# A masked decay on VectorE, whole-chunk weight splits on GpSimd, and earlier decode queries in a hybrid decoder layer

## The reference

```python
h = rmsnorm(x); p = h @ w_in        # q-latent | kv-latent | rope key | z | x,B,C | dt | gates
A = mla_attend(...)                 # 16 heads, causal for the prompt, over 2048 cached positions for samples
# SSD branch, 32 heads in 8 groups of 4, chunks of 128 tokens
cs = cumsum(dt * a)                 # per chunk and head
decay = exp(where(tri, cs[l] - cs[s], -inf))
y_diag = (C B^T * decay) @ (x * dt)
state  = state * exp(cs_end) + B^T (x * dt * exp(cs_end - cs))
y_off  = C @ state * exp(cs)        # samples: one step with exp(dt * a) and dt
B_out = rmsnorm_by_group((y + D x) * silu(z))
mix = (sigmoid(ga) * (A @ w_a) + sigmoid(gb) * (B_out @ w_b)) @ w_out
x = x + rmsnorm(mix);  x = x + rmsnorm(w_down relu(w_up rmsnorm(x))^2)
```

## Time and profile before

| | |
|---|---|
| time, median of 3 runs | 1741.69 us (1738.41 to 1745.32) |
| profiled execution, own time | 1741.69 us |
| its span, first to last instruction | 1739.9 us |
| TensorE busy, mean granted clock | 1517.3 us (87%), 0.913 of full speed |
| VectorE busy | 893.5 us (51%) |
| ScalarE busy | 512.4 us (29%) |
| GpSimd busy | 586.4 us (34%), of it line 413: 574.3 us, 736 instructions, 811 ns each |
| GpSimd idle before line 413, waiting for ScalarE's rounding | 1106.1 us |
| TensorE line 572, 256 instructions | 36.9 us busy |
| TensorE line 623, 64 instructions | 12.3 us busy |

### The profile page before, as it was taken

The page is one execution under the profiler, slowest core; times in us unless marked ns, Lnnn a source line. Parts: engine busy times, 40 slices in busy tenths (PEclk is TensorE's granted clock), DMA queues, the critical chain, the costliest instruction groups (busy, mean ns, idle before and its releaser), DMA issues.

```text
span 1739.9 us, 29329 instructions
## 1 busy us (share of the span) xinstructions
PE 1517.3 (87%) x11936; PEld 1405.3 (81%) x11936; DVE 893.5 (51%) x1794; ACT 512.4 (29%) x930; POOL 586.4 (34%) x748
## 2 busy tenths in 40 slices
PE   5799989899797997989987688998993999999995
PEld 4798778788686887878876467878993999999995
DVE  5566677666675776757767432221336222222225
ACT  3232323323233232332332222222222322222221
POOL 2353332233322323324231012323443454544541
PEclk9898989899898998998988688997995999999997
DMA  3133122122221212212213059863320223223221
GB/s 111 61 94 96 49 80 68 46 88 63 78 73 41 88 61 85 77 44 87 63 44 106 4 179 286 270 206 115 126 95 13 83 88 97 86 98 97 86 98 61
DMA packets 109592, 160.51 MB, mean 92 GB/s; under 512 B 16498, under 2 KB 83571, under 8 KB 109459
## 3 DMA queue, kind: packets, MB, share of 16 engines
q1 hardware_dynamic: 56594, 130.14, 23.1%
q10 hardware_dynamic: 52864, 28.51, 5.8%
HBM read 145.87 MB, written 12.74 MB: 91 GB/s over the span
## 4 chain that ended last, share of the span: by engine, by line
PE 72%; DVE 18%; ACT 3%; issue 3%; ACTq 1%; SPq 1%; POOL 1%; DMA 1%; DVEq 0%; POOLq 0%
PE lin L456 53%; PE lin L631 2%; PE Pb L487 2%; PE lin L495 2%; PE Pb L543 2%; PE lin L605 2%; DVE acc L1467 1%; PE Pb L552 1%; PE lin L572 1%; ACTq L1027 1%; PE Pb L584 1%; PE Pb L587 1%; PE Pb L559 1%; DVE arena L1281 1%; DVE arena L1363 1%
## 5 line engine op out<-in xcount | busy, mean ns | idle before, releaser
L413 POOL TENSOR_TENSOR w_lo<-w_stage,w_hi 128x256 fp32r<-128x256 f32 x736 | 574.3, 811 | 1106.1 <-ACT w_hi L826 1106.1
L456 PE MATMUL lin<-act_hi,w_hi 128*128 128x260 f32 x1760 | 373.5, 295 | 22.2 <-DVE acc L1535 10.8
L456 PE MATMUL lin<-act_lo,w_hi 128*128 128x260 f32 x1760 | 362.1, 288 | 0.0
L456 PEld LDWEIGHTS lin<-act_hi,w_hi 128*128 128x128 f32 x1760 | 279.5, 195 | 31.8 <-issue 24.5
L456 PEld LDWEIGHTS lin<-act_lo,w_hi 128*128 128x128 f32 x1760 | 280.7, 195 | 0.0
L826 ACT ACTIVATE w_hi<-w_stage 128x1024 fp32r<-128x1024 f32 x184 | 193.9, 1054 | 257.4 <-PE lin L456 221.1
L456 PE MATMUL lin<-mid_hi,w_hi 128*128 128x260 f32 x1024 | 218.7, 296 | 34.1 <-DVE mid_lo L1456 18.8
L456 PE MATMUL lin<-act_hi,w_lo 128*128 128x260 f32 x1760 | 233.4, 285 | 0.0
L456 PEld LDWEIGHTS lin<-act_hi,w_lo 128*128 128x128 f32 x1760 | 219.5, 189 | 3.3 <-issue 3.3
L456 PE MATMUL lin<-mid_lo,w_hi 128*128 128x260 f32 x1024 | 214.1, 292 | 0.0
L456 PEld LDWEIGHTS lin<-mid_hi,w_hi 128*128 128x128 f32 x1024 | 166.7, 199 | 44.8 <-issue 35.8
(11 more groups left out here) (238 smaller groups left out, 2006.5 us busy)
## 6 DMA issues: line engine op xcount, KB each, us to landing
w_stage<-in_wall SPq DMA_DIRECT2D x184, 512.0 KB, 3.7
arena<-in_cache SPq DMA_DIRECT2D x124, 144.0 KB, 3.2
arena<-in_state ACTq DMA_DIRECT2D x16, 512.0 KB, 7.5
out_stateT<-arena ACTq DMA_DIRECT2D x16, 512.0 KB, 4.0
o_attn<-in_cache SPq DMA_DIRECT2D x64, 128.0 KB, 3.6
o_attn<-in_cache ACTq DMA_DIRECT2D x64, 128.0 KB, 3.9
arena<-in_xT SPq DMA_DIRECT2D x8, 520.0 KB, 5.6
out_yT<-arena SPq DMA_DIRECT2D x8, 260.0 KB, 2.0
```

The source lines that it names most:

```text
L413: low = pool.tensor_tensor(w_lo[:, slot, part], w_stage[:, slot, part], w_hi[:, slot, part].bitcast(F32), ALU.subtract)
L456: mm = pe.matmul(lin[:, pl.slot, hf, 0:HALF], w[:, ch.slot, off:off + P], r[:, hf * HALF:(hf + 1) * HALF], start=(k == 0 and p == 0), stop ...
```

## The change

It has three parts. First, GpSimd's split of a chunk is one instruction of 1024 columns in place of four of 256. Second, the head rows are no longer picked by matmuls against `ident`: VectorE multiplies `cs3`, repeated four times, by the one-hot columns of the group's heads into `csm` (32x512, one per scan chunk) and `sdm` (32x64, one per group), and one matmul against ones spreads them. The mask of chunk c + 1 is made at the end of VectorE's `scan_front(c)`, the first one and `sdm` at the group's start. Third, in a decode row `queries(b + 1)` stands before `row_out(b - 1)`.

```diff
@@ semaphores csm_ready, sdm_ready; tiles @@
+        csm = sb("csm", [SSM_HEADS, HPG, CHUNK])
+        sdm = sb("sdm", [SSM_HEADS, HPG, 16])
@@ gpsimd, split @@
-                        for q in range(4):
-                            part = slice(256 * q, 256 * q + 256)
-                            low = pool.tensor_tensor(w_lo[:, slot, part], w_stage[:, slot, part],
-                                                     w_hi[:, slot, part].bitcast(F32), ALU.subtract)
-                        low.then_inc(S["w_split"], 1)
+                        pool.tensor_tensor(w_lo[:, slot, :], w_stage[:, slot, :], w_hi[:, slot, :].bitcast(F32),
+                                           ALU.subtract).then_inc(S["w_split"], 1)
@@ tensor, scan_front(c) @@
+                    pe.wait_ge(S["csm_ready"], g * 4 + (c + 1))
-                    for h in range(HPG):
-                        pe.matmul(lin[:, pl.slot, 0, h * P:(h + 1) * P], head_row(h), cs3[:, tok], start=True, stop=True)
+                    pe.matmul(lin[:, pl.slot, 0, :], ones[0:32, :], csm[:, :, :], start=True, stop=True)
@@ tensor, decode decays @@
-                if g:
-                    pe.wait_ge(S["state_ready"], g * 4)
-                else:
-                    pe.wait_ge(S["rows_ready"], 1)
-                    pe.wait_ge(S["sp_ln"], 2)
-                for h in range(HPG):
-                    mm = pe.matmul(Pb[:, 3, 16 * h:16 * h + 16], head_row(h), cs3[:, SEQ:SEQ + 16], start=True, stop=True)
-                mm.then_inc(S["sdec_mm"], 1)
+                pe.wait_ge(S["sdm_ready"], g + 1)
+                pe.matmul(Pb[:, 3, 0:64], ones[0:32, :], sdm[:, :, :], start=True, stop=True
+                          ).then_inc(S["sdec_mm"], 1)
@@ vector, group @@
+                onehot = ident[0:32, bass.ds(g * 4, 4)]
+
+                def masked_decay(c):
+                    dve.tensor_tensor(csm[:, :, :], repeat(cs3[:, CHUNK * c:CHUNK * (c + 1)], HPG),
+                                      spread(onehot, CHUNK), ALU.mult).then_inc(S["csm_ready"], 1)
@@ vector, end of scan_front(c) @@
+                    if c < NCH - 1:
+                        masked_decay(c + 1)
@@ vector, start of the group's rest @@
+                dve.tensor_tensor(sdm[:, :, :], repeat(cs3[:, SEQ:SEQ + 16], HPG), spread(onehot, 16), ALU.mult
+                                  ).then_inc(S["sdm_ready"], 1)
+                masked_decay(0)
@@ vector, row(b) @@
                 dve.tensor_scalar(sms[:, 1:2], sms[:, 0:1], -SM_SCALE, None, ALU.mult).then_inc(S["s_bias"], 1)
+                if b < NB - 1:
+                    queries(b + 1)
                 if b:
                     row_out(b - 1)
...
-                if b < NB - 1:
-                    queries(b + 1)
```

More of the change, by code:

```diff
@@ L149 @@
     hist_in conv_out raw_act conv_acc conv_tanh xc_ready qbd_hi_s q_ready k_act v_act
-    sdec_mm st_in0 st_in1 st_new st_out0 st_out1 scores max_bias exp_done prob_ready
-    pt_done pt_ready pv_done o_ready a_row a_seg a_exp b_ready y_done state_ready state_out
+    sdm_ready sdec_mm st_in0 st_in1 st_new st_out0 st_out1 scores max_bias exp_done prob_ready
+    pt_done pt_ready pv_done o_ready csm_ready a_row a_seg a_exp b_ready y_done state_ready state_out
     yg_ready sqg_ready g_stat g_diag g_val g_hi g_ready z_tanh groups_over
@@ L561, in values @@
                     mm.then_inc(S["pv_done"], 1)
-                def head_row(h):
-                    return ident[0:32, 4 * g + h:4 * g + h + 1].to_broadcast([32, P])
                 def scan_front(c):
```

## The result

The changed kernel takes 1798.3 us (median of 4 runs, 1794.1 to 1803.8) against 1740.1 (4 runs, 1734.5 to 1745.3) of the kernel before on the same chip: ratio 1.034, 95% interval 1.029 to 1.038. It is slower, as forecast, but by 58 us, where 33 were forecast; the time lies 0.3 us outside the range. The profiled execution has a span of 1796.4 us against 1739.9, a difference of 56.5.

What follows compares the result with a forecast made beforehand. The prediction took TensorE as the bound (72% of the chain, VectorE 18%), mostly waiting for VectorE. Steady groups 25.9, first and last group 0 and decode rows 7.2 made +33.1 on 1741.69: about 1775 us, range 1748 to 1798.

Steps and rivals of the forecast that it cites:

- Part 1: GpSimd's split as one instruction: 2.37 us long, 0.45 less than four quarters, shutting VectorE's SBUF-only work out for 2.1 us.
- Part 2: Steady groups: masks wait out the split, 3.1 us a group over the chunks; blocked branch sums add 1.7 us.
- Part 3: Fewer TensorE matmuls: 1.0 us a group saved at the decode decays, 0.1 at the head rows.
- the sum of the steady groups: Blocking less TensorE savings in each steady group: 3.7 us, seven groups 25.9 us.
- TensorE's clock lost: Rival: longer second-chunk waits bring one more lower-clock stretch per group, +22 us in seven groups, 1797 us; chance 12%.
- clock gained: Rival: fewer matmuls at the decode decays end the present lower-clock stretch, -22 us, 1753 us; chance 10%.
- The first and last group at 0: First and last group: few splits in their chunks, added VectorE 0.68 against saved 1.0; taken as 0, ends -2 and +3.
- Part 4: Decode rows: moved queries push the second line 1501 behind a split, TensorE 1.8 us late in four rows, +7.2 us.
- The rest: Feed-forward part: its VectorE instructions with two SBUF inputs do not run while a split does; left at nothing.
- VectorE goes first: Rival: the mask slips in ahead of the queued split, 2.2 us a group for 3.1, 1769 us; within the forecast's 58%.
- decode rows spared: Rival: a 16-column instruction with two tensors slips through in the decode rows, 1768 us; within the forecast's 58%.
- ports handed over inside: Rival: GpSimd lets VectorE in during its instruction, blocking stays 0.4 us, only savings remain, 1733 us; chance 14%.

Runs made afterwards that it cites:

- experiment 3: The changed kernel with GpSimd's split in two halves of 512 columns instead of one instruction; ratio 1.016 to the kernel before.
- experiments 6: The changed kernel with unused matmuls cut to fit TensorE's waits in the second and third scan chunk; ratio 1.0256 to the kernel before.
- experiment 7: The kernel before with two unused VectorE products behind Cx in the second chunk, lengthening TensorE's wait there; ratio 1.010 to the kernel before.
- experiment 4: The changed kernel with the decode rows' queries back behind the mix weights; ratio 1.0315 to the kernel before.
- experiment 10: The kernel before with only the sample mask sdm and its one matmul added, replacing four matmuls; 1720.7 us, ratio 0.993.

## Why the prediction was right in direction and short in size

- **Part 1, blocking of 2.1 us.** Right: 2.16 on the masks, 2.0 on the convolution tap; the doses of experiment 3 confirm the mechanism.
- **Part 2, where it falls.** Right in place, too high in size. TensorE's standing time grew by 1.8 us in the second chunk (forecast 1.9), 0.5 in the third (0.6), 0.2 in the first (0.6), 1.1 from the last Cx to the decays (1.6 at the branch sums' wait itself, forecast 1.7) and 0.4 from there to the first Cx: +3.9 a group where 4.8 were forecast. In two of the 21 places the first Cx is the one that is blocked (2.56, 2.9) and not the mask: GpSimd got in first. It changes little, since both stand one behind the other. In three groups the fourth Cx is blocked as well (2.9), which the forecast did not have.
- **Part 3, TensorE's savings.** 0.8 to 1.1 a group, for 1.1.
- **The step that failed** first is the sum of the steady groups, "3.7; seven of them 25.9", which left the clock where it was. Measured are 40.9: the clock cost 18 to 21 us, and the waits were 6 us less than forecast. The rival "TensorE's clock lost" had the term right: 22 us in seven groups. That its total of 1797 meets the 1796.4 of the span is luck, since the shorter waits and the term of the next point cancel. It had a chance of 12%, against 10% for a clock gained. I took it for a coin toss ("No row here says which of the two"), but it was not symmetric once waits of about 2 us were added at three places in a group: experiments 6 and 7 show what such waits bring. One execution each stands behind the 123.5 and 166.4, but the kernel of experiment 4, with the same groups as the changed one, has 171.0, and that of experiment 7 has 122.9 outside the chunk where its wait is. The place was off, too: one stretch per group was expected in the second chunk; in fact they lie behind three of the waits, each in about half of the groups. The rival's other half was real as well: with fewer matmuls at the decays the stretch there ends (experiment 10), but in no kernel with the whole split.
- **The first and last group at 0** is the second term that failed, with ends of -2 and +3. Measured are +4.6 and +6.3, 10.9 us of the 23.4 by which the profiled execution missed the forecast. Up to the first decays, the five kernels with the changed kernel's code took 144.3 to 146.8, the three with the code of before 136.4 to 142.2. In every kernel with the whole split TensorE waits 2.3 us there for `qbd_lo`, which VectorE makes; with quarters it is 0.7 at most. So at least 1.6 us of the loss comes with the whole split, in a place that the forecast did not look at. In the last, half-speed time is 68.3 us for 53.2, half of which excess would be 7.6, and TensorE stands 1.7 us longer; the other kernels with all masks took 100 to 109 us there, those without 98 to 106, so the share of the change in it is not shown.
- **Part 4, the decode rows**: +5.8 for 7.2, near in size, in part by luck. It is the first instruction of line 1503 that is blocked, not the second, and in all six rows (2.36 for 0.23), not four; the waits are 1.3 us on average and not 1.8. By experiment 4 the move costs something with quarters, too.
- **The rest** was left at nothing and gave -1.1. Right.
- **The rivals "VectorE goes first", "decode rows spared" and "ports handed over inside"** are out, by the masks of 2.83 us, line 1503 and experiment 3.

## What to carry over

A long GpSimd instruction kept VectorE's SBUF-only work out for nearly its whole length here (2.16 of 2.38 us), so splitting it in short ones was worth more than the 0.45 us a chunk that the single instruction saves on an engine with time to spare. Look for the VectorE instructions that stand behind the trigger of the split, and whether TensorE waits behind them. When a change lengthens TensorE's waits, add the clock to the sum: here 18 to 21 us on 28 us of waits. It is a chance and not a threshold: waits of 1.6 to 2.6 us had a half-speed stretch behind them in some groups and not in others. Where such waits can't be removed, fillers that end before the wait does give a part of it back. Measure one filler first, count half-speed time only where TensorE works, and ask which engine it will wait for once it is faster.

## What the runs showed of the hardware that I had not expected

- A half-speed stretch of 3.4 us costs 1.2 to 1.6 us when dense matmuls lie under it, and much less when waits do: the 90.9 us taken away at the groups' ends gave back 11.1. The Trainium skill, page "TensorE: Matmul & The Clock Gate", section "Terms", prices such time at half of itself; by that, as an estimate, the fillers would have given 45 us. The chunks nearly agree with the page, and so does the work at the groups' ends, 23 us faster for 52.8 us of half-speed time. The 38 us in which TensorE stood still do not, and there the measurement decides.
- The same program with the same waits gets the stretch in two of seven groups (experiment 7). The runs of the kernel before spread from 1724 to 1748 us over the study, so one profiled execution is only one draw of it.
